# Five places of TensorE's order refilled, and an expert's weight loads moved ahead of a store, in a decoder trunk with 16 experts

## The reference, cut to what matters

```python
x = x + concat([forgetting_attention, hgrn2_recurrence, conv]) @ w_out      # 8 heads of 64 attend; w_out is 1024x1024
q = rmsnorm(x) @ w_xq;  k, v = split(rmsnorm(mem) @ w_xkv)                 # 256 memory tokens
x = x + softmax(q @ k.T * s) @ v @ w_xo                                    # 4 heads of 256
h = rmsnorm(x)
x = x + sum over experts e of weight[t, e] * ((silu(h @ w_gate[e]) * (h @ w_up[e])) @ w_down[e])
return rmsnorm(x)
```

## Time and profile before

| | |
|---|---|
| median of 3 runs | 707.51 us (707.44 to 708.28) |
| the profiled execution's own time | 706.44 us |
| its span, first to last instruction | 704.5 us |
| PE busy | 679.5 us, 96% of the span |
| DVE, ACT, POOL busy | 281.8, 144.2, 78.5 us |
| DMA | 111.90 MB, 159 GB/s in the mean |
| granted TensorE clock, mean | 0.995 of full speed |

### The profile page before, as it was taken

The page is one execution under the profiler, slowest core; times in us unless marked ns, Lnnn a source line. Parts: engine busy times, 40 slices in busy tenths (PEclk is TensorE's granted clock), DMA queues, the critical chain, the costliest instruction groups (busy, mean ns, idle before and its releaser), DMA issues.

```text
span 704.5 us, 8433 instructions
## 1 busy us (share of the span) xinstructions
PE 679.5 (96%) x3398; PEld 332.3 (47%) x3398; DVE 281.8 (40%) x669; ACT 144.2 (20%) x308; POOL 78.5 (11%) x106
## 2 busy tenths in 40 slices
PE   7999999999999999999999999999999999999993
PEld 4644445453547665444444555545565333333331
DVE  3107599936143665213221312323344821212156
ACT  3011351003053444211001112211111010101013
POOL 3000081412020000000000000000001011110062
PEclk9999999999999999999999999999999999999997
DMA  8803240302136523300019310630029999999773
GB/s 289 312 0 120 72 167 1 120 1 80 42 119 185 180 66 115 120 1 0 1 38 395 105 58 1 238 120 30 31 92 345 363 372 392 374 376 390 284 235 123
DMA packets 69939, 111.90 MB, mean 159 GB/s; under 512 B 5648, under 2 KB 43780, under 8 KB 69900
## 3 DMA queue, kind: packets, MB, share of 16 engines
q1 hardware_dynamic: 65724, 96.16, 39.5%
q0 software_dynamic: 4176, 15.21, 5.8%
HBM read 101.90 MB, written 9.46 MB: 158 GB/s over the span
## 4 chain that ended last, share of the span: by engine, by line
PE 87%; DMA 5%; DVE 3%; SPq 2%; ACT 1%; issue 1%; POOL 1%; DVEq 0%; POOLq 0%
PE bank L1925 25%; PE bank L2207 16%; PE bank L1800 11%; PE bank L1935 6%; PE bank L1829 5%; PE bank L2257 2%; PE bank L1971 2%; PE bank L2277 2%; PE bank L2160 2%; PE bank L1957 2%; DMA W<-y_dram,A 1%; PE bank L1782 1%; PE bank L2147 1%; PE bank L2043 1%; DMA x_sb<-in_x_dram 1%; PE bank L2068 1%
## 5 line engine op out<-in xcount | busy, mean ns | idle before, releaser
L1925 PE MATMUL bank<-hT,W 128*128 128x512 f32 x368 | 160.6, 593 | 0.9 <-DVE hT L1081 0.9
L2207 PE MATMUL bank<-W,n_sb 128*128 128x512 f32 x256 | 114.2, 596 | 0.0
L1925 PEld LDWEIGHTS bank<-hT,W 128*128 128x128 f32 x368 | 69.4, 190 | 84.9 <-issue 83.1
L1800 PE MATMUL bank<-W,A 128*32 128x512 f32 x672 | 84.8, 594 | 1.7 <-DVE A L1172 1.5
L2207 PEld LDWEIGHTS bank<-W,n_sb 128*128 128x128 f32 x256 | 47.3, 190 | 52.4 <-issue 52.3
L1435 DVE SCALAR_TENSOR_TENSOR A<-A,pc 128x511 f32<-128x511 f32 (+29 forms) x60 | 51.6, 860 | 2.0
L695 POOL TENSOR_TENSOR rstd<-ss,mhalf 128x1 f32<-128x1 f32 x14 | 7.7, 550 | 362.8 <-DVE ss L1065 200.0
L1800 PEld LDWEIGHTS bank<-W,A 128*32 128x32 f32 x672 | 23.6, 110 | 49.4 <-issue 47.4
L1829 PE MATMUL bank<-Dn,A 128*32 128x512 f32 x264 | 36.3, 595 | 0.0
L906 ACT ACTIVATE A<-bank 128x512 f32<-128x512 f32 (+1 forms) x22 | 12.2, 557 | 113.0 <-PE bank L1925 77.0
L1287 DVE TENSOR_TENSOR A<-A,bank 128x256 f32<-128x256 f32 x12 | 5.1, 421 | 70.7 <-ACT A L825 70.7
(11 more groups left out here) (307 smaller groups left out, 813.5 us busy)
## 6 DMA issues: line engine op xcount, KB each, us to landing
W<-in_w_gate_dram SPq DMA_DIRECT2D x14, 1024.0 KB, 12.7
W<-in_w_up_dram SPq DMA_DIRECT2D x14, 1024.0 KB, 14.5
Dn<-in_w_down_dram SPq DMA_DIRECT2D x11, 1024.0 KB, 13.6
W<-in_w_in_dram SPq DMA_DIRECT2D x5, 2048.0 KB, 9.2
W<-in_w_xkv_dram SPq DMA_DIRECT2D x4, 2048.0 KB, 8.2
hT<-in_w_down_dram SPq DMA_DIRECT2D x5, 1024.0 KB, 13.4
y_dram<-A POOLq DMA_DIRECT2D x10, 512.0 KB, 7.1
W<-in_w_out_dram SPq DMA_DIRECT2D x2, 2048.0 KB, 7.8
```

Source lines behind the costliest of these rows:

```text
L1800: mm = nc.tensor.matmul(PS[2 + b][r, :], xgT[:, b, c, r], gu_at[GU_HOME[e]][:, c, :], start=c == 0, stop=c == DC - 1)
L1925: mm = nc.tensor.matmul(bank[0:w, 0:n], lhs, src[:, c, 0:n], start=c == 0, stop=c == DC - 1)
L2207: mm = nc.tensor.matmul(PS[(k + (2 if base else 0)) % 4][:, :], src[:, c, t * P:(t + 1) * P], W[:, (n_load + n) % SLOTS, c, :], start=firs ...
```

## The change

No arithmetic is added or removed. Chunks of products, one VectorE addition and some DMA issues stand at other places in their engines' streams:

1. SP: `decay_sums(sp, 1)`, the decay sums of the second pair of heads, is issued ahead of load 9 and the four router loads, not behind them.
2. PE: chunks 6 and 7 of output product 0 are done at `u == UNITS`, ahead of `pv(13)`.
3. PE: the last two chunks of the last memory product follow the transposes of the last tile.
4. PE: the first two chunks of `x_query(2)` stand ahead of the first score products.
5. DVE: `add_half(0, 1)` directly follows `add_half(0, 0)`.
6. SP: the gate and up weights of TAKEN[2] are issued after the 15th output product, not after the 16th; the gate weights of TAKEN[3] take their place ahead of the last rows' store.

```diff
-            sp.wait_ge(*freed(14))
-            load_gate(sp, TAKEN[2])
+            sp.wait_ge(wout_ps, 15)
+            load_gate_up(sp, TAKEN[2])
+
+            sp.wait_ge(wout_ps, 16)
+            load_gate(sp, TAKEN[3])
             store_rows(ST - 1)
-            load_up(sp, TAKEN[2])
-            load_gate_up(sp, TAKEN[3])
+            load_up(sp, TAKEN[3])
             load_gate_up(sp, TAKEN[4])
...
                 if n >= SLOTS:
 
                     sp.wait_ge(*freed(n - SLOTS))
+                if n == 9:
+
+                    sp.wait_ge(ho_step, 2 * HP)
+                    decay_sums(sp, 1)
...
-
-                    sp.wait_ge(ho_step, 2 * HP)
-                    decay_sums(sp, 1)
             experts_loads(sp)
...
                 add_half(t, 0)
+                if t == 0:
+                    add_half(t, 1)
                 route_evac(t, 0)
                 if t:
                     place(t - 1)
                 first_mean(t)
-                add_half(t, 1)
+                if t:
+                    add_half(t, 1)
...
                 if u < UNITS:
                     qk(u)
+                if u == UNITS:
+                    pe.wait_ge(s_done, 2 * (UNITS - 1))
+                    pe.wait_ge(ho_step, 4)
+                    pe.wait_ge(co_done, 2)
+                    loaded(pe, 10)
+                    project_some(0, 10, catT, 0, [6, 7], last=False)
                 if u >= PV_LAG:
                     pv(u - PV_LAG)
...
+            def last_memory(chunks):
+
+                g = XQ0 - 1
+                if chunks[0] == 0:
+                    loaded(pe, 9)
+                    bank_free(pe, g)
+                for c in chunks:
+                    mm = nc.tensor.matmul(PS[bank_of(g)][:, :], memT[:, c, (MT - 1) * P:MT * P], W[:, 1, c, :], start=c == 0, stop=c == DC - 1)
+                if chunks[-1] == DC - 1:
+                    mm.then_inc(proj, 1)
...
                         pe.wait_ge(x1_done, 5)
-                        run([along(1, MT - 1, 0, 512, src=memT)], XQ0 - 1, 9)
+                        last_memory(range(6))
                     if t >= 1:
                         turn_tile_pe(stage, t - 1, nA)
+                last_memory(range(6, DC))
...
-            project_some(0, 10, catT, 0, order, last=False)
+            project_some(0, 10, catT, 0, order[2:], first=False, last=False)
...
                 x_query(2 * h + 1)
                 if h:
                     x_turn(h - 1)
+                else:
+                    x_query(2, range(2))
                 x_scores(h * ST)
                 x_scores(h * ST + 1)
                 if h < XH - 1:
-                    x_query(2 * h + 2)
+                    x_query(2 * h + 2, range(0 if h else 2, DC))
```

More of the change, by code:

```diff
@@ L2186, in project_memory @@
                 return g
[L2188 to L2200, removed]
             def project_some(base, n_load, src, k, chunks, first=True, last=True):
@@ L2210, in project_some @@
                     mm.then_inc(wout_ps, 1)
+            g = project_memory(0, g)
+            pe.wait_ge(proj_out, XKV0)
+            for u in range(UNITS + TURN_LAG):
+                if u < UNITS:
+                    qk(u)
+                if u == UNITS:
[4 more added lines that the diff above has]
+                    project_some(0, 10, catT, 0, [6, 7], last=False)
+                if u >= PV_LAG:
+                    pv(u - PV_LAG)
+                if u >= TURN_LAG:
+                    pt(u - TURN_LAG)
+                if u and pair_end(u - 1) is not None:
+                    fox_ms(pair_end(u - 1))
+                if u in KV_AT:
+                    g = project_memory(KV_AT.index(u), g)
+            def last_memory(chunks):
[7 more added lines that the diff above has]
+                    mm.then_inc(proj, 1)
             def project_out(base, n_load, src, order, stage, begun=0):
@@ L2247, in _, with x_query @@
             pe.wait_ge(x1_done, 8)
-            def x_query(c):
-                run([across(c // 4, P * (c % 4))], XQ0 + c, 12 + c // 4)
+            def x_query(q, chunks=range(DC)):
+                g = XQ0 + q
+                if chunks[0] == 0:
+                    loaded(pe, 12 + q // 4)
+                    bank_free(pe, g)
+                for c in chunks:
+                    mm = nc.tensor.matmul(PS[bank_of(g)][:, :], W[:, q // 4, c, P * (q % 4):P * (q % 4) + P], hT[:, c, :], start=c == 0, stop=c == DC - 1)
+                if chunks[-1] == DC - 1:
+                    mm.then_inc(proj, 1)
             def x_scores(u):
```

## The result

The changed kernel takes 702.26 us (701.49 to 702.66 over 4 runs) against 707.48 us for the kernel before on the same chip: a ratio of 0.9923 [0.9906, 0.9941], 5.2 us faster. The prediction was 702.7 us.

What follows compares the result with a forecast made beforehand. TensorE, busy 679.5 of 704.5 us, was taken as the bound. Gains 0.88 + 1.11 + 0.85 + 1.73 + 0.20 = 4.77 us off 707.51 gave 702.74, about 702.7 us, range 702.1 to 703.6.

Steps and rivals of the forecast that it cites:

- Edit 1: 0: First pair of heads: earlier decay sums gain nothing; the 1.26 us wait stays, being ACT's behind two exponentials.
- The bound of 1.1 us for late sums: Upper bound on the earlier decay sums' gain, if they land later in other executions than in the profiled one.
- Edit 2: 0.88: End of the mixer, ahead of `pv(13)`: two moved chunks remove TensorE's wait, worth 0.88 us, between 0.80 and 0.97.
- Edit 3: 1.11: Ahead of the first queries: splitting the last memory product removes TensorE's wait, worth 1.11 us, between 0.94 and 1.11.
- Edit 4: 0.85: Ahead of the first scores: two chunks of the third query product fill TensorE's wait, 0.85 us, between 0.69 and 0.85.
- Edit 5: 1.73: Ahead of the second half tile's turn: DVE's earlier second addition removes TensorE's wait, 1.73 us, between 1.56 and 1.73.
- The margin of the additions: Time by which DVE's two additions finish before TensorE turns the first half tile: 0.3 to 0.7 us.
- Edit 6: 0.20: Ahead of the eleventh expert pass: weights 5.5 us earlier against TensorE remove its 0.20 us idle.
- The store: Last rows' store, now behind three loads, still in time: 0.3 us of earlier loads left, against 1.1 us of slack.
- the pair ahead of it: Two 1 MB loads issued after the 15th product, expected to land 8.4 us after the first issue.
- the case: Both earlier loads still ahead of the last rows' store: store 5.5 us later, 4.4 beyond slack, 707.1 us; chance 0.03.
- The sum: Whole kernel: the edits' gains add to 4.77 us (4.19 by bracketed idle), giving about 702.7 us; chance 0.62.

Runs made afterwards that it cites:

- the pair still there: Changed kernel with expert 1's gate and up loads issued after the 16th output product, three loads directly ahead of the store: 708.9 us, ratio 1.0029.
- two steps later: Changed kernel plus memory-product chunks before turn 4's values and row-choice chunks before the last half tile, decay-sum and weight-load moves undone: 700.96 us, ratio 0.9919.

## Why the prediction was right

- **What bounds it.** Right. TensorE's busy time stayed within 0.8 us, and nearly all of the 5 us are four waits that closed.
- **Edit 1: 0.** Right: 1.26 became 1.24, and undoing the edit moved neither the first nor the twelfth pass by 0.01 us. The bound of 1.1 us for late sums in other executions was not needed.
- **Edit 2: 0.88.** `pv(15)` starts at 304.86 and started at 305.85, behind the 14 records of the earlier trace rows. Less the 0.08 us by which this execution was ahead at the earlier trace rows, that is 0.91.
- **Edit 3: 1.11.** The queries start at 366.14 instead of 368.24; 2.10 less the 0.91 and 0.08 is 1.11.
- **Edit 4: 0.85.** Too small: 1.05. From the first queries to the second scores it is 388.47 - 366.14 = 22.33 us, and 23.38 before (to 391.62). Beside the wait, the first row of scores is 1.89 us long, against 1.99 in the earlier trace rows: the first products behind an idle stretch took longer themselves. The other tenth is of the same kind and belongs to edit 3's wait: the queries' row is 14.00 us long for 32 records in the earlier trace rows, and 15.61 for 36 here, less four of 0.429 is 13.89. I had priced the waits and not the restarts.
- **Edit 5: 1.73.** 1.78 in the trace, 1.79 alone. The margin of the additions was 0.8 us, a little above what I gave it.
- **Edit 6: 0.20.** 0.27 in the trace, 0.26 alone, 0.19 when undone. The size is right and the step behind it is not. I had the weights 5.5 us earlier at the eleventh pass, by moving 2 MB forward in the stream, and named as a sign that they land over 4 us ahead of it. They land 1.4 us ahead with edit 1 undone, and as the pass starts with edit 6 alone. What I left out is SP's wait for the first pass to free homes, which takes most of the head start back. That 0.20 came out is partly luck, since any lead above it gives the same, and the wait was also gone once without the edit.
- **The store.** Right that it is not late, because the pair ahead of it has left by then. Two readings were off, both on the safe side. The 15th product does not end at 515.32, since four records of the 16th stand ahead of that row: SP's first load left 1.5 us ahead of the row's counterpart (508.86 against 510.38) and 9.6 us ahead of the third load, not 8.1. And the store's slack was 2.1 us, not 1.1, as DVE waits for the row choice and not only for the pass table. With the pair still there the extra delay is 6.6 us where I estimated 5.5, of which 4.25 reached the first pass as against my 4.4: that near a hit is luck, since the delay and the slack were both a microsecond too small. What I had missed is the clock: 2.8 us on top, so that the case came out at 708.9 and not at 707.1. The Trainium skill ("DMA: Bandwidth & Descriptors", Queues, rings and completion order) has each engine take one ring's descriptors in order, and this run agrees: 9.9 us with three loads ahead and 3.3 with one.
- **The sum.** 4.77 was forecast; the five measured terms make 5.12, and the landmarks 5.13. Of the difference 0.2 us are the restarts. The median moved by 5.25 (707.51 to 702.26) and the profiled execution by 4.47, with a tail longer by 0.6. Of the 1.07 us by which the earlier median lay above its profile, which I carried over, 0.29 are left; that the median hit within half a microsecond owes something to scatter of that size.

## What to carry to other kernels

When an engine that sets the time waits for a short chain, move in only as much independent work as the wait needs: here two chunks (1.72 us) against waits of 0.7 to 1.0. What is moved in is taken from a neighbour's cover. Twice as much was harmless at edit 2's place, where that cover was long, and three and four times as much at the other two opened new waits of 1.06 and 0.53. Price a wait by start to start, restart included, not by the idle figure alone. An edit on a queue that is worth nothing today can be what lets the next gain through: earlier weights were worth 0.3 us at most here and 1.5 us two steps later. And a head start in a stream of loads counts only up to the next place at which the stream itself waits: 5.5 us were put in here, and at most 1.5 were left 120 us on.

## What the hardware showed that I had not expected

- **A wait can cost more than its length.** Behind 5.05 us of idle the granted clock was 0.50 (the 1.2 GHz level of the two) for the next 6 us, and one pass took 9.89 us in place of 7.07. Behind the waits of up to 1.57 us shown here the rows are at most 0.1 us longer than without a wait. With five filler products in the wait the clock stayed at 1.00. The Trainium skill ("TensorE: Matmul & The Clock Gate", Part 1) has these two levels, with the lower one after idleness; the trace agrees.
- **A small store behind large loads.** 512 KB landed in 3.3 us behind one load of 1 MB, and also behind three of which the first two had been issued over 13 us earlier, and in 9.9 us when all three had been issued within the 4.2 us ahead of it.
- **Scatter of equal work.** The first 215 us of the program differ by 1.6 us between executions, with the wait for the first weights, and the eight gathers at the end by 1.7 us. Both are above several of the terms measured here, which is why those were read from landmarks.
